# Swapping two steps of a gated-linear-attention chain and the two half banks of PSUM behind them

## Chip, core and metric

The kernel runs on one core of one Trainium2 chip. The metric is the device time of one execution in microseconds; the time before is the median of three executions.

## What is computed

One decoder layer with two branches side by side, on 1024 prompt tokens and 8 x 8 sample tokens: forgetting attention (with a paged cache of 4096 past tokens per sample) and gated linear attention (GLA), merged by gates. The change lies in the GLA branch. Cut to what matters, per head and chunk of 64 tokens:

```python
q_in, k_in = qc * exp(b), kc * exp(-b)                   # b: running sum of log decay
att = where(causal, q_in @ k_in.T, 0)                    # scores
o   = att @ vc + q_in @ S                                # output, S the 128 x 256 state
S   = exp(b_last) * S + (kc * exp(b_last - b)).T @ vc    # state
y   = rmsnorm(o) * silu(gg)                              # norm over 256, gate
```

## The kernel before, in words

Each engine runs its own list of instructions in order; engines meet at semaphores. `schedule()` writes one list of steps for all engines, and each engine runs its handler for every step that concerns it (`run`). The list mixes three streams: the parts of the weight projections (`z`, 6 matmuls each: a quarter of a 128-row weight tile by one of three token chunks of 384, 384 and 320 columns), the decode attention (`kt` transposes a pair of K pages on VectorE, `sc` 64 small score matmuls, `pt` two transposes on TensorE with a copy on ScalarE, `pv` 64 small matmuls, `new`, `soft`, `exp`, `od` the softmax and output of one sample), and the GLA chain. In `gla_steps()` the chain of a head is a list `slow`, and `mix` puts the same number of projection steps (`quick`) behind each of its members, as far as they divide evenly. Some of these have no TensorE part (`evac`, `ev_y`, `ev_z`: sigmoid work on ScalarE and VectorE), so a slot can hold nothing for TensorE.

The chain of head i, block t (128 tokens, two chunks), is

- `att`: TensorE writes the scores (L2028) into bank 7, columns 0 to 127. VectorE masks them in two operations, a minimum (L1826, reads the bank, signals `att_min`) and a maximum (L1828, signals `att_set`).
- `u`: TensorE writes the two state updates (L2035) into columns 0 to 255 of banks 2 and 7. It waits for `att_min` of this block, for `gated` of the block before and for the old state. VectorE folds them into the state (L1843, two operations).
- `o`: TensorE writes the output (L2042, L2045) into bank 7, columns 256 to 511. ScalarE squares and sums it (L1644) and makes the factor of the norm (L1646, L1648).
- `on`: VectorE scales the output into `o_n` (L1849, signals `on_set`).
- `og`: TensorE turns `o_n` (two transposes, L2053) into bank 2, columns 256 to 511; VectorE multiplies both halves with the gate (L1863, L1865, signals `gated`).

After eight blocks come the steps of the sample tokens: `satt` (VectorE first copies q into `q_sp`, L1873, four operations; TensorE writes scores, L2060; VectorE masks them and spreads the keys, L1878), `so`, `son`, `sog`. Also on VectorE's list stand the splitting of each weight tile into a high and a low part (L264, behind ScalarE's L259; it is run at part 1 of the first chunk of a tile, so at every step `z` n 0 1) and L1671, the transposition of K pages.

Semaphore names as used below: `on_set`, `gated`, `att_min`, `qd_set` (the copies into `q_sp`). "Head 1 block 6" counts from 0.

## Time and profile before

| | us |
|---|---|
| median of three executions | 1595.02 |
| lowest, highest of the three | 1590.8, 1600.67 |
| the profiled execution | 1588.89 |
| its span in the profile | 1587.2 |
| TensorE busy in it | 1447.4 (91%) |
| VectorE busy | 726.3 (46%) |
| ScalarE busy | 565.3 (36%) |

The span is the time between the first and the last instruction of the profiled execution; its own time is 1.7 us more. The profiled execution is faster than any of the three that the median is taken over. The GLA chains of the four heads run from 553 to 656, 745 to 858, 949 to 1050 and 1139 to 1233 us of the span.

### The profile page before, as it was taken

How to read it: one execution, taken by the hardware profiler on the slowest of the kernel's cores; microseconds unless marked ns; L12 is line 12 of the kernel's file. 1: busy time of each engine (PE TensorE's matmuls, PEld its weight loads, DVE VectorE, ACT ScalarE, POOL GpSimd, SP SyncE). 2: the span in 40 equal slices, each digit the busy share in tenths (PEclk: the TensorE clock that was granted, in tenths of full speed). 3: DMA queues.
4: the chain of work that ended last, by engine and by line, in shares of the span. 5: the costliest groups of instructions: out<-in, count | busy, mean ns of one | idle time of the engine just before them, and what ended most of it. 6: DMA issues, size and time to landing. Idle time of an engine off the chain costs nothing. (4 is left out here: it accounts for less than half of the span.)

```text
span 1587.2 us, 43486 instructions
## 1 busy us (share of the span) xinstructions
PE 1447.4 (91%) x16281; PEld 1226.6 (77%) x16281; DVE 726.3 (46%) x1578; ACT 565.3 (36%) x1311; POOL 528.7 (33%) x953
## 2 busy tenths in 40 slices
PE   5999898989978897999989999889998899999998
PEld 5878777777767876788877888768876798888876
DVE  4344353543636555655546545655554223333221
ACT  6343444444532334323443334423334353111100
POOL 4444434440047135344353534454251122111000
PEclk9989999999989999999999999989999999999999
DMA  5131301222238688899997999879985764321521
GB/s 173 32 85 34 85 24 54 72 58 68 55 114 212 189 233 216 225 238 235 239 248 206 263 244 243 219 217 244 231 198 158 224 249 139 108 101 62 167 92 60
DMA packets 153411, 250.51 MB, mean 158 GB/s; under 512 B 45897, under 2 KB 58826, under 8 KB 152690
## 3 DMA queue, kind: packets, MB, share of 16 engines
q1 hardware_dynamic: 121618, 215.68, 49.8%
q0 software_dynamic: 31584, 32.04, 7.3%
q8 instruction: 131, 2.15, 0.6%
q14 instruction: 78, 0.64, 0.1%
HBM read 217.37 MB, written 30.22 MB: 156 GB/s over the span
## 5 line engine op out<-in xcount | busy, mean ns | idle before, releaser
L289 PE MATMUL psum<-h_hi,w_hi 128*128 128x384 f32 (+1 forms) x1344 | 491.0, 365 | 13.8 <-DVE q_fm L915 3.5
L289 PE MATMUL psum<-h_hi,w_lo 128*128 128x384 f32 (+1 forms) x1344 | 446.9, 332 | 0.0
L289 PE MATMUL psum<-h_lo,w_hi 128*128 128x384 f32 (+1 forms) x1344 | 446.4, 332 | 0.0
L1457 POOL DMA_DIRECT2D sc<-tmp_bias x512 | 278.3, 549 | 256.7 <-PE psum L1943 252.6
L289 PEld LDWEIGHTS psum<-h_hi,w_hi 128*128 128x128 f32 x1344 | 258.3, 192 | 67.1 <-issue 48.0
L289 PEld LDWEIGHTS psum<-h_lo,w_hi 128*128 128x128 f32 x1344 | 259.4, 193 | 2.7 <-issue 0.5
L289 PEld LDWEIGHTS psum<-h_hi,w_lo 128*128 128x128 f32 x1344 | 257.9, 192 | 0.0
L678 POOL DMA_DIRECT2D lfp<-in_cache_logf x256 | 124.1, 485 | 176.1 <-issue 176.1
L1671 DVE STREAM_TRANSPOSE k_page<-k_page 128x1024 f32<-128x1024 f32 x128 | 156.1, 1232 | 28.8 <-DMA k_page<-in_cache_k 27.8
L264 DVE TENSOR_TENSOR w_lo<-w_raw,w_hi 128x1024 fp32r<-128x1024 f32 x63 | 76.8, 1219 | 110.6 <-ACT w_hi L259 110.5
L259 ACT ACTIVATE w_hi<-w_raw 128x1024 fp32r<-128x1024 f32 x63 | 66.1, 1049 | 69.3 <-DMA w_raw<-in_w_tiles 37.9
L1958 PE MATMUL psum<-v_page,p_t 128*32 128x64 f32 x4096 | 75.2, 227 | 9.8 <-issue 9.6
L1958 PEld LDWEIGHTS psum<-v_page,p_t 128*32 128x32 f32 x4096 | 63.9, 114 | 24.3 <-issue 23.9
L1924 PEld LDWEIGHTS psum<-k_page,q_row 128*32 128x32 f32 x4096 | 64.8, 116 | 22.6 <-issue 22.2
L1924 PE MATMUL psum<-k_page,q_row 128*32 128x64 f32 x4096 | 75.5, 229 | 5.5 <-issue 5.4
L2376 PE MATMUL psum<-o_hi,w_hi 128*128 128x384 f32 (+1 forms) x192 | 69.1, 360 | 0.0
L2368 PE MATMUL psum<-fox_o,up_a 128*128 128x384 f32 (+1 forms) x192 | 62.5, 468 | 0.4 <-issue 0.4
L2376 PE MATMUL psum<-o_hi,w_lo 128*128 128x384 f32 (+1 forms) x192 | 62.6, 326 | 0.0
L2376 PE MATMUL psum<-o_lo,w_hi 128*128 128x384 f32 (+1 forms) x192 | 62.6, 326 | 0.0
L813 ACT ACTIVATE prob<-prob,nmin 128x128 f32<-128x128 f32 (+7 forms) x64 | 49.5, 773 | 36.1 <-DVE nmin L955 36.1
L2291 ACT ACTIVATE h_hi<-g_pair 128x384 fp32r<-128x384 f32 (+1 forms) x24 | 12.1, 505 | 133.2 <-DVE g_pair L2325 133.2
L124 ACT ACTIVATE sig<-sig 128x384 f32<-128x384 f32 (+1 forms) x54 | 27.2, 504 | 90.2 <-DVE sig L130 90.2
(259 smaller groups left out, 2142.4 us busy)
## 6 DMA issues: line engine op xcount, KB each, us to landing
k_page<-in_cache_k SPq DMA_DIRECT2D x256, 256.0 KB, 3.8
v_page<-in_cache_v SPq DMA_DIRECT2D x256, 256.0 KB, 4.9
w_raw<-in_w_tiles SPq DMA_DIRECT2D x63, 512.0 KB, 5.6
g_pair<-tmp_gates SPq DMA_DIRECT2D x16, 544.0 KB, 4.6
sc<-tmp_bias POOLq DMA_DIRECT2D x512, 16.0 KB, 4.4
tmp_ogla<-gate POOLq DMA_DIRECT2D x4, 1088.0 KB, 6.8
g_pair<-tmp_ogla SPq DMA_DIRECT2D x8, 544.0 KB, 7.3
x_in<-in_x_prompt SPq DMA_DIRECT2D x8, 512.0 KB, 6.1
```

The costliest lines, as they stand in the source:

```text
L124: inc(act.activation(g, g, ACT.Exp), "g_sig")
L259: act.activation(self.hi[:, k % 2], self.raw[:], ACT.Copy).then_inc(self.hi_set, 1)
L264: dve.tensor_tensor(self.lo[:, k % 2], self.raw[:], self.hi[:, k % 2].bitcast(F32), ALU.subtract).then_inc(self.lo_set, 1)
L289: m = pe.matmul(out, wt[:, s, k, :], h[:, k, t0:t0 + w], start=(k == 0 and a == 0), stop=(k == KT_ - 1 and a == 2))
L678: pool.dma_start(lfp[a % P:a % P + 1, a // P, :], ins["cache_logf"][ds(page, 1)] .rearrange("o p h -> o (p h)")).then_inc(lf_in[a // P], 16)
L813: inc(act.activation(p, p, ACT.Exp, bias=nmin[:, t % 2, hh:hh + 1], scale=-1.0, accum_out=den[:, t % 2, hh:hh + 1]), "exp_set")
L1457: pool.dma_start(dst, src.unsqueeze(0).to_broadcast([TS, 2, 256])).then_inc(sc_in[j % SLOTS], 16)
L1671: inc(dve.transpose(both, both), "kt_set")
L1924: m = MM(bank[4 + e][32 * hp:32 * hp + 32, col:col + HD].rearrange("p (g t) -> p g t", g=2), q_row[:, b, :], k_page[:, slot:slot + 2, 32 * ...
L1958: m = MM(bank[6][32 * hp:32 * hp + 32, e * HD:(e + 1) * HD], p_t[:, g % 2, col:col + 32], v_page[:, g % 2, tb, h * HD:(h + 1) * HD], start ...
L2368: m = pe.matmul(bank[2 + c][:, 0:w], up_a[:, j % 2, k, :], fox_o[:, k, t0:t0 + w], start=(k == 0), stop=(k == NA - 1))
L2376: m = pe.matmul(bank[5 + c][:, 0:w], wt[:, s, k, :], v[:, k, t0:t0 + w], start=(k == 0 and a == 0), stop=(k == NBR - 1 and a == 2))
```

## The change

The order of the steps: the scores of block t+1 (for the last block: of the sample) stand before the turning of block t. The positions in the list stay, so the projection steps between them stay where they are too; `att` and `og` exchange their places. The output `o` goes to bank 2, columns 256 to 511, and the turned output to bank 7, columns 256 to 511. TensorE's waits follow: `att` waits for `gated` of block t-2 in place of the norm; `og` of block t waits in addition for `att_min` of block t+1; `satt` waits for `gated` of block 6, no longer of block 7.

```diff
-        chain = [[((name, i, t), cost) for name, cost in (("att", 0.3), ("u", 0.55), ("o", 1.0), ("on", 0), ("og", 0.25))] for t in range(TT)]
-        sample = [(("satt", i), 0.3), (("so", i), 1.3), (("son", i), 0), (("sog", i), 0.25)]
+        chain = [[(("att", i, 0), 0.3)]] + [[] for t in range(TT)]
+        for t in range(TT):
+            chain[t] += [(("u", i, t), 0.55), (("o", i, t), 1.0), (("on", i, t), 0)]
+            chain[t].append((("att", i, t + 1) if t < TT - 1 else ("satt", i), 0.3))
+            chain[t + 1].append((("og", i, t), 0.25))
+        sample = chain[TT] + [(("so", i), 1.3), (("son", i), 0), (("sog", i), 0.25)]
...
             def ostat(i, t):
                 W(act, "ot_mm", i, t)
-                inc(A(o_n[:], bank[7][:, DV:2 * DV], ACT.Square, accum_out=ost[:, 0:1]), "ss_set")
+                inc(A(o_n[:], bank[2][:, DV:2 * DV], ACT.Square, accum_out=ost[:, 0:1]), "ss_set")
...
             def o_norm(i, t):
-                inc(dve.tensor_scalar(o_n[:], bank[7][:, DV:2 * DV], ost[:, 2:3], None, ALU.mult), "on_set")
+                inc(dve.tensor_scalar(o_n[:], bank[2][:, DV:2 * DV], ost[:, 2:3], None, ALU.mult), "on_set")
...
             def og(i, t):                                   # VectorE
-                    turned = bank[2][:, DV + j * P:DV + (j + 1) * P]
+                    turned = bank[7][:, DV + j * P:DV + (j + 1) * P]
...
             def att_step(i, t):                             # TensorE
-                W(pe, "on_set", i, t)
+                W(pe, "gated", i, max(t - 1, 0))
                 inc(MM(bank[7][:, 0:P], k_in[:, tok], q_in[:, tok], start=True, stop=True), "att_mm")
...
             def o_step(i, t):
-                o = bank[7][:, DV:2 * DV]
+                o = bank[2][:, DV:2 * DV]
...
             def og(i, t):                                   # TensorE
                 W(pe, "on_set", i, t + 1)
+                W(pe, "att_min", i, min(t + 2, GTS))
-                    m = pe.transpose(bank[2][:, DV + j * P:DV + (j + 1) * P], o_n[:, j * P:(j + 1) * P], cc("ident"))
+                    m = pe.transpose(bank[7][:, DV + j * P:DV + (j + 1) * P], o_n[:, j * P:(j + 1) * P], cc("ident"))
...
             def satt(i):
-                W(pe, "gated", i, TT)
+                W(pe, "gated", i, TT - 1)
...
             def so(i):
-                o = bank[7][:, DV:2 * DV]
+                o = bank[2][:, DV:2 * DV]
```

Five stretches of the list, in the order before; the change exchanges the two steps in brackets and leaves all others (`z` n c p: tile n, chunk c, part p).

```
head 0, blocks 3, 4:  o 3; pt; pv; z 0 1; ev_y; on 3; z 0 2; [og 3]; ev_z; kt; z 0 3; [att 4]; kt; z 1 0; u 4
head 0, blocks 6, 7:  z 0 1; kt; o 6; ev_y; z 0 2; on 6; ev_z; kt; [og 6]; z 0 3; sc; [att 7]; z 1 0; evac; u 7
head 1, blocks 6, 7:  o 6; z 2 1; on 6; z 2 2; [og 6]; kt; z 2 3; kt; z 0 0; [att 7]; sc; z 0 1; u 7
head 1, sample:       on 7; z 1 0; od; kt; z 1 1; [og 7]; ev_y; kt; z 1 2; [satt]; ev_z; sc; z 1 3; so
head 3, blocks 2 to 7: on 2; z; ev_y; pv; [og 2]; z; z; kt; [att 3]; u 3; kt; z 0 0; sc; o 3; evac; on 3; z 0 1;
                      [og 3]; ev_y; [att 4]; z 0 2; pt; u 4; pv; o 4; z; on 4; z; [og 4]; pt; [att 5]; evac; u 5;
                      sc; z; o 5; on 5; new; z; [og 5]; ev_z; soft; pv; [att 6]; z; u 6; z; pt; pv; o 6; on 6; z;
                      [og 6]; [att 7]; ev_y; u 7
```

## Rows read from the trace of the kernel before

**Rows 1.** The waits of PE, whole span: us in total, times, longest.

```profile
...
PE psum L2053 <- DVE o_n L1849: 14.7, 14, 3.4
...
PE psum L2035 <- DVE con L1826: 4.9, 6, 2.4
...
PE psum L2060 <- issue: 3.9, 2, 2.1
...
PE psum L2060 <- DVE q_sp L1873: 2.1, 1, 2.1
...
```

**Rows 2.** Busy time, clock and DMA of two stretches (the columns stand in the first line).

```profile
core 0: us, PE busy (x) PEld busy (x) DVE busy (x) ACT busy (x) POOL busy (x), PEclk, DMA share, GB/s
1046.00:1139.00 93.00, 89.43 (x1486) 79.14 (x1485) 51.47 (x102) 29.41 (x71) 40.24 (x74) 0.96 0.93 235
1139.00:1233.00 94.00, 81.06 (x1291) 61.84 (x1288) 47.70 (x124) 36.67 (x107) 24.39 (x45) 0.96 0.73 184
```

**Rows 3.** Timeline, head 3, blocks 3 and 4: start, us, engine, line.

```profile
...
1182.85 0.65 PE L2045 MATMUL psum<-state,q_in 128*64 128x256 f32 x4
...
1184.68 0.48 DVE L1849 TENSOR_SCALAR o_n<-psum,ost 128x256 f32<-128x256 f32 x1 [2.47 <-issue]
...
1185.31 0.41 PE L2053 MATMUL psum<-con,o_n 128*128 128x128 f32 x2 [0.54 <-DVE o_n L1849]
...
1186.90 1.22 DVE L264 TENSOR_TENSOR w_lo<-w_raw,w_hi 128x1024 fp32r<-128x1024 f32 x1 [1.73 <-ACT w_hi L259]
...
1189.25 0.29 DVE L1826 TENSOR_TENSOR con<-psum,con 128x128 f32<-128x128 f32 x1 [0.21 <-DVE sig L130]
...
1189.60 0.70 PE L2035 MATMUL psum<-gv_tok,gk_tok 64*128 64x256 f32 x4 [2.38 <-DVE con L1826]
...
```

**Rows 4.** Timeline, head 0, block 6.

```profile
...
631.76 1.24 DVE L1671 STREAM_TRANSPOSE k_page<-k_page 128x1024 f32<-128x1024 f32 x1
...
633.60 0.48 DVE L1849 TENSOR_SCALAR o_n<-psum,ost 128x256 f32<-128x256 f32 x1 [0.23 <-DVE sig L130]
...
634.23 0.66 PE L2053 MATMUL psum<-con,o_n 128*128 128x128 f32 x2 [3.43 <-DVE o_n L1849]
...
638.01 0.49 PE L2028 MATMUL psum<-q_in,k_in 128*128 128x128 f32 x2
...
```

**Rows 5.** Timeline, head 1, block 7 and the sample's scores.

```profile
...
843.40 0.48 DVE L1849 TENSOR_SCALAR o_n<-psum,ost 128x256 f32<-128x256 f32 x1 [3.20 <-ACT ost L1648]
...
848.65 0.41 DVE L1873 COPY q_sp<-q_in 128x32 f32<-128x32 f32 x4
...
849.16 0.66 PE L2060 MATMUL psum<-q_sp,k_in 128*64 128x128 f32 x2 [2.14 <-DVE q_sp L1873]
...
```

**Rows 6.** Timeline, other waits of PE, and one turning with its gate.

```profile
...
601.61 0.41 PE L2053 MATMUL psum<-con,o_n 128*128 128x128 f32 x2 [1.20 <-DVE o_n L1849]
...
604.29 0.70 PE L2035 MATMUL psum<-gv_tok,gk_tok 64*128 64x256 f32 x4
...
833.10 0.41 PE L2053 MATMUL psum<-con,o_n 128*128 128x128 f32 x2 [1.10 <-DVE o_n L1849]
...
833.81 0.34 DVE L1865 TENSOR_SCALAR gate<-psum,vec 128x128 f32<-128x128 f32 x1
...
835.26 0.38 PE L2028 MATMUL psum<-q_in,k_in 128*128 128x128 f32 x2
...
1039.90 0.50 PE L2060 MATMUL psum<-q_sp,k_in 128*64 128x128 f32 x2 [2.13 <-issue]
...
```

**Rows 7.** Three stretches behind a wait, columns as in rows 2.

```profile
...
634.50:637.00 2.50, 2.50 (x20) 2.06 (x22) 1.22 (x3) 0.15 (x1) 1.33 (x3) 0.50 0.47 157
849.70:853.20 3.50, 3.50 (x72) 3.03 (x71) 2.37 (x8) 0.00 (x0) 0.49 (x1) 0.62 0.85 242
1040.30:1045.20 4.90, 4.90 (x83) 2.78 (x82) 1.82 (x7) 0.00 (x0) 0.14 (x1) 0.50 0.78 206
...
```

**Rows 8.** The waits of DVE from 550 to 1240 us.

```profile
...
DVE k_page L1671 <- DMA k_page<-in_cache_k: 8.2, 9, 2.1
...
```

## Prediction

> **What bounds the kernel now.** I read the page first: TensorE is busy for 1447.4 of 1587.2 us, VectorE for 726.3. What can be gained without taking matmuls away is TensorE's idle time. The waits of TensorE come second [rows 1]: the turning (L2053) waited 14 times for the norm, 14.7 us in all; the state update (L2035) 6 times for the mask's minimum, 4.9 us; the sample's scores (L2060) three times, 3.9 + 2.1 = 6.0 us. One of the 14 norm waits, 2.7 us, is the sample's own (`sog` of head 3), which the change leaves alone. So 12.0 + 4.9 + 6.0 = 22.9 us are within its reach. Third the table by stretch [rows 2]: between two GLA chains (1046 to 1139 us) TensorE is busy for 89.4 of 93.0 us, in the chain of head 3 for 81.1 of 94.0. That chain has the fewest projection parts between its steps.
>
> Then the timeline, to see what each wait is made of. In head 3 block 3 the output ends at 1182.85 + 0.65 = 1183.50 and the turning starts at 1185.31: the norm takes 1.81 us from matmul to matmul, and its wait is short, 0.54 us [rows 3]. The long waits have another cause: VectorE works its list in order, and the norm stands in it behind the splitting of a weight tile (1.22 us, which itself waits for ScalarE) and K transpositions (1.24 us each). In head 0 block 6 they push the norm to 633.60, 3.43 us of waiting for a chain whose bare length is 1.81 us [rows 4]. The sample's scores wait for copies (0.41 us) that stand behind a transposition in the same way: they begin at 848.65, long after the norm at 843.40 [rows 5]. VectorE is half idle on average and late at these places.
>
> A wait also costs afterwards. Behind those of 3.43, 2.14 and 2.13 us the granted clock was 0.50, 0.62 and 0.50 for 2.5, 3.5 and 4.9 us, so at or partly at the 1.2 GHz level [rows 7]. The loss is 2.5 x 0.50 = 1.3, 3.5 x 0.38 = 1.3 and 4.9 x 0.50 = 2.5 us.
>
> **What the change adds and removes.** No instruction is added or removed on any engine, and the bytes are the same. TensorE's and VectorE's lists, and the few issues that POOL makes at `att` and `satt` (state in and out, not waited for in these chains), have two steps exchanged. The scores no longer wait for the norm: they and the slot behind them now cover it. Added are two waits. The turning waits for the minimum of the next block's mask, which on VectorE stands behind the norm; queued behind the turning on TensorE are the next projection part and the state update. The state update waits, as before, for the gate of the block before, but that gate now lies one slot ahead of it, not two.
>
> The prices from rows: a projection part is (835.26 - 833.10 - 0.14)/2, about 1.0 us, where 0.14 is what two transposes take of the array when nothing stops them (estimate from the two-part slot of [rows 6]). The minimum is 0.29 us [rows 3]. From the start of the turning to the end of the gate's second operation 833.81 + 0.34 - 833.10 = 1.05 us pass [rows 6]. So a slot with one projection part just covers the gate, and an empty slot leaves 1.05 - 0.41 = 0.64 us of waiting.
>
> Block by block, by the order in the list (section on the change). *Waits that go whole*: head 1 block 6. The norm ends at 832.95, TensorE came at 833.10 - 1.10 = 832.00 [rows 6]. Now it runs scores and two parts first and comes to the turning after 834.0, when norm and minimum (833.3) are over: -1.1. The same order holds for head 2 blocks 4 and 6 (0.26, 0.87) and head 3 block 0 (0.41): together -2.6.
>
> *Waits that go in part*: head 0 block 3 and head 2 block 3 (1.20, 1.29). In the first the norm ends at 601.61 - 0.15 = 601.46 (0.15 us from the norm's end to the turning, as in [rows 3]). The turning can start at 601.8, but the gate now stands on VectorE behind mask (0.6) and one transposition (1.24), and ends at 601.46 + 0.6 + 1.24 + 0.6 = 603.9. The state update starts there; with the wait it had started at 604.29 [rows 6]. So -0.4 each, -0.8, instead of -2.5.
>
> *Head 0 block 6*: norm until 634.08, then a transposition, then the minimum: 634.08 + 1.24 + 0.3 less the overlap = 635.5. TensorE has scores, one part and 64 score matmuls (1.1) and comes at 633.1, so it waits 2.4 us instead of 3.43. The state update then starts at 636.8 to 637.9 (with and without full clock), against 638.01 + 1.5 = 639.5 [rows 4]: -1.6 to -2.7. A wait of 2.4 us is as long as those that brought the clock down, so part of the slow stretch returns behind the update: I take -1.2.
>
> *Sample's scores*: they move ahead of the last turning, and the copies ahead of one or two transpositions. In head 1 the norm ends at 843.88; before the copies VectorE had two transpositions, the gate (0.6), a sigmoid product (0.5) and its own waits, until 848.65 [rows 5]; now transposition, gate and sigmoid product of the last 2.2 us stand behind them, so they end near 849.06 - 2.2 = 846.9. TensorE, which came at 849.16 - 2.14 = 847.0 behind turning and part, comes 1.3 us earlier, at about 845.7, and waits some 1.3 us instead of 2.14. That is -0.8, and with a wait so much shorter I count the slow stretch of 1.3 us as gone: -2.1. In head 2 the copies can't pass the gate multiplications of the projection (1.1 us) and a decode product; the wait is 2.1 us as before [rows 6], the clock likely falls again, but two transpositions (2.4 us) now overlap with the two parts that follow (2.0 us), of which the slow clock takes a part back: -1.3. In head 0 the same with a wait of 1.8 us: -0.6. Together -4.0.
>
> *What gets worse*: blocks 3 and 4 of head 1 have a transposition between mask and gate: the state update comes 0.25 us later each, +0.5. In head 3, blocks 2 to 7, several slots are empty. Block 2's turning is directly followed by the update: wait 0.64 in place of 0.38 plus the order, +0.2. Block 3 is the critical one: scores at 1185.0, but the minimum behind norm and split (until 1188.12 + 0.2) ends at 1188.6. The turning has nothing ahead of it and waits 3.5 us, where before 0.54 and 2.38 us were waited [rows 3]; the update comes at 1190.2 instead of 1189.60, while the slow stretch that followed may move or stay: 0 with 1.5 us to either side. Blocks 4 and 5 add 0.6 and 0.1 (slots without a part). In blocks 6 and 7 ScalarE's exponentials and VectorE's fixed sum of work before the product of decode set the pace as before, so that +0.9 is taken up there. Head 3: 0, from -2 to +3.
>
> Sum: -2.6 - 0.8 - 1.2 - 4.0 + 0.5 + 0 = -8.1 us of 22.9 within reach.
>
> **Does DMA take it back?** Between the chains the mean DMA share is 0.93 [rows 2], which reads as nearly full; yet VectorE waited only 8.2 us in nine waits for K pages from 550 to 1240 us [rows 8], all hidden from TensorE. Pages are loaded when score matmuls free them, so a faster chain asks for them earlier by at most 1%. I take 0.5 us for it, between 0 (all hidden, as these nine) and 8 (every such wait comes on top).
> The Trainium skill ("Perfetto Trace Analysis", section Identifying the Most-Contended Engine) says that the occupancy of the 16 DMA engines misleads and that bytes per second are to be judged; with its aggregate of about 435 GB/s (section Roofline) the 235 GB/s of this stretch leave much room, and the DMA term would be 0 (an estimate by that page). By the share alone the whole gain would be lost. The short waits for pages stand nearer to the page's reading.
>
> So the profiled execution of 1588.89 us becomes about 1588.9 - 8.1 + 0.5 = 1581 us. It was 6 us faster than the median; on the median's footing the forecast is 1595.0 - 7.6, about 1587 us.
>
> **Rivals.**
> *More goes than I count (nearly the whole 22.9 us).* If VectorE's backlog shrinks as a whole because its waits for the turning vanish, all three waits go, and 5 us of slow clock: -25, 1570 us. For it: the scores wait for nothing now. Against: the norm remains in front of the mask on VectorE, and the turning waits for both.
> *The wait only changes its name.* The turning waits for the minimum where it waited for the norm, the update for the gate where it waited for the minimum; VectorE's list has the same sum. Head 3 is such a case by my own working. If heads 0 and 2 behave like it: 0 to -3, 1593 us. DMA as the bound gives the same time.
> *Slower.* The mechanism: the gate now one slot ahead of the state update. It decides where that slot holds less than 1.05 us for TensorE or where VectorE has a transposition between mask and gate. If it bites in 14 of the 28 inner blocks at 0.64 us, that is +9, and two more falls of the clock at 1.3 to 2.5 us make +13, with nothing saved: 1608 us. Against it: most slots hold a part and a `kt` that VectorE has finished.
>
> **Numbers.** Forecast (gain 3 to 15 us) 0.58; name only 0.20; more 0.12; slower 0.10. A measurement of this kernel can tell about 1%, 16 us. Faster by more than that needs nearly all of "more" and some of the forecast's upper end: 0.14. Slower by more than 1% is a part of the last rival: 0.06. Within 1%: 0.80. The range takes the forecast's bounds (-15 to -3), the name-only case and the median's own scatter (1590.8 to 1600.7), so about 5 us on each side: 1575 to 1599 us.
>
> **What would show it.** TensorE's waits at L2053 for `o_n` fall from 14.7 to under 6 us, but new ones for L1826 appear there (about 2.4 us in head 0 block 6, 3.5 in head 3 block 3). L2035 waits for L1865 in place of L1826, 4 to 7 us. The three waits at L2060 stay near 1.8, 1.4 and 2.1 us, now directly behind the last norm. The stretch of head 3's chain keeps its 94 us within 2. I am wrong if L2053's waits for both causes stay above 12 us, or fall below 4, or if TensorE begins to wait for K pages.

## The result and the profile after

| | before | after |
|---|---|---|
| median of 12 executions each, run in turns | 1596.83 | 1585.95 |
| lowest, highest | 1587.23, 1602.16 | 1578.24, 1606.22 |
| profiled execution, its own time | 1588.89 | 1586.29 |
| its span | 1587.2 | 1584.6 |

The ratio of after to before is 0.9939, 95% interval 0.9911 to 0.9967. It leaves out executions more than 1.5% above the fastest of their kernel (here the one of 1606.22), and it isn't the quotient of the two medians, here or below. The same changed kernel was measured twice more beside the experiments: 0.9971 (0.9938 to 1.0004) and 0.9948 (0.992 to 0.9975). The mean of the three is 0.9953, so 7.5 us of 1596. The forecast was 7.6 us, and 1587 us for the median, which came out at 1585.95. The change makes the kernel about half a per cent faster, less than single executions of one kernel differ.

The lines moved by four (from the turning on by five): scores L2032, update L2039, output L2046, turning L2058, sample's scores L2065, the mask's minimum L1830, norm L1853, gate L1867 and L1869, copies into `q_sp` L1877, the decode's score matmuls L1928 (before L1924) and value matmuls L1962 (L1958). First the page of after, its span and the busy times:

```profile
...
span 1584.6 us, 43485 instructions
...
PE 1441.8 (91%) x16281; PEld 1223.6 (77%) x16281; DVE 725.9 (46%) x1578; ACT 565.8 (36%) x1311; POOL 530.7 (33%) x953
...
```

TensorE is busy for 5.6 us less than before (1441.8 against 1447.4) with the same 16281 matmuls, and 2.6 us of span are gone. This pair alone would say that time at the slower clock went. Two more profiles of each kernel (below) don't bear it out: TensorE is busy for 1447.4, 1443.7 and 1440.4 us in before and for 1441.8, 1446.7 and 1447.6 us in after. Next the waits of TensorE of after, from 550 to 1240 us, where the GLA chains lie: us in total, times, longest. They answer to [rows 1], whose waits all lie in this stretch too.

```profile
...
PE psum L2039 <- issue: 7.1, 9, 2.1
...
PE psum L2065 <- issue: 6.2, 4, 2.2
...
PE psum L2058 <- DVE con L1830: 5.6, 4, 3.4
...
PE psum L2058 <- DVE o_n L1853: 2.7, 1, 2.7
...
```

The turning waits for the norm only once, 2.7 us: that is the sample's own turning in head 3, which the change leaves alone. In place of the other thirteen it waits four times for the minimum, 5.6 us. The update waits 7.1 us. The view calls this "issue"; by the timeline the gate's last operation is what each of these updates follows. The sample's scores wait in all four heads, 6.2 us. Here are the same sums for the three profiles of each kernel that I have by the end (before: the one of the prediction and two more; after: the first and two repeats), with the 0.2 us of "issue" at the turning:

| waits of TensorE, 550 to 1240 us | before | after |
|---|---|---|
| turning, norm or minimum | 14.7, 15.9, 17.2 | 8.5, 10.0, 9.9 |
| update | 4.9, 5.3, 5.3 | 7.1, 7.4, 6.1 |
| sample's scores | 6.0, 6.2, 6.0 | 6.2, 6.2, 6.2 |
| sum | 25.6, 27.4, 28.5 | 21.8, 23.6, 22.2 |
| score and value matmuls of the decode | 10.0, 11.7, 10.2 | 16.5, 11.1, 16.7 |
| all waits of TensorE | 51.6, 56.1, 53.6 | 53.4, 51.0, 58.1 |

At the three places on which the change acts, 27.2 us become 22.6 on average. The decode's own matmuls wait 4.1 us longer, and the sum of all waits is the same, 53.8 and 54.2 us. So by these profiles TensorE doesn't wait less in this stretch; the chain gets through it faster, as the table of the chains shows below.

The place that the forecast held for the worst is head 3 block 3, here in the timeline of after (start, us, engine, line; in brackets how long the engine waited and for what). It answers to [rows 3].

```profile
...
1179.93 0.38 PE L2032 MATMUL psum<-q_in,k_in 128*128 128x128 f32 x2
...
1182.21 1.22 DVE L264 TENSOR_TENSOR w_lo<-w_raw,w_hi 128x1024 fp32r<-128x1024 f32 x1 [1.73 <-ACT w_hi L259]
...
1183.36 0.28 DVE L1830 TENSOR_TENSOR con<-psum,con 128x128 f32<-128x128 f32 x1
...
1183.74 0.41 PE L2058 MATMUL psum<-con,o_n 128*128 128x128 f32 x2 [3.43 <-DVE con L1830]
...
1185.76 0.63 PE L1947 MATMUL psum<-con,sc 128*128 128x128 f32 x2
...
1186.32 1.22 PE L2039 MATMUL psum<-gv_tok,gk_tok 64*128 64x256 f32 x4
...
```

The scores are done at 1180.3, and the turning stands directly behind them. The minimum that it needs (L1830, 1183.36) is queued behind the split of a weight tile (L264), which itself waited 1.73 us for ScalarE; so TensorE stands for 3.43 us. In before this place cost 0.54 us at the turning and 2.38 at the update. The transposes at 1185.76 take 0.63 us and the update 1.22, where an update takes 0.70 at the full clock.

### The profile page after: what moved, and what is told of

It reads as the page before. It is cut to its first block, busy times and chain, and to the rows that moved or that the text cites. A ratio compares the mean times of both kernels' runs of the same rounds, so it can differ in the third digit from the quotient of the medians.

```text
span 1584.6 us, 43485 instructions
## 1 busy us (share of the span) xinstructions
PE 1441.8 (91%) x16281; PEld 1223.6 (77%) x16281; DVE 725.9 (46%) x1578; ACT 565.8 (36%) x1311; POOL 530.7 (33%) x953
## 4 chain that ended last, share of the span: by engine, by line
PE 54%; issue 5%; DMA 4%; DVE 3%; SPq 2%; ACT 2%; POOL 1%; DVEq 0%; ACTq 0%
PE psum L289 25%; PE psum L2381 6%; PE psum L1962 4%; PE psum L2373 4%; PE psum L1928 4%; PE psum L2411 3%; DMA w_raw<-in_w_tiles 3%; PE psum L2039 1%; PE psum L2046 1%; PE psum L2049 1%; PE psum L1947 1%; SPq L1402 1%; DMA k_page<-in_cache_k 1%; PE psum L2009 1%; PE psum L2420 1%
## 5 line engine op out<-in xcount | busy, mean ns | idle before, releaser
L264 DVE TENSOR_TENSOR w_lo<-w_raw,w_hi 128x1024 fp32r<-128x1024 f32 x63 | 76.8, 1219 | 108.3 <-ACT w_hi L259 108.2
L259 ACT ACTIVATE w_hi<-w_raw 128x1024 fp32r<-128x1024 f32 x63 | 66.1, 1049 | 72.9 <-DMA w_raw<-in_w_tiles 50.2
L1962 PE MATMUL psum<-v_page,p_t 128*32 128x64 f32 x4096 | 73.3, 222 | 14.1 <-issue 14.0
L1962 PEld LDWEIGHTS psum<-v_page,p_t 128*32 128x32 f32 x4096 | 61.9, 111 | 29.1 <-issue 28.8
L1928 PEld LDWEIGHTS psum<-k_page,q_row 128*32 128x32 f32 x4096 | 62.4, 112 | 21.7 <-issue 21.5
L1928 PE MATMUL psum<-k_page,q_row 128*32 128x64 f32 x4096 | 73.1, 224 | 5.0 <-issue 4.8
L1510 ACT ACTIVATE p_t<-psum 128x256 f32<-128x256 f32 x64 | 24.2, 378 | 100.7 <-PE psum L1947 100.7
L2296 ACT ACTIVATE h_hi<-g_pair 128x384 fp32r<-128x384 f32 (+1 forms) x24 | 12.1, 506 | 133.2 <-DVE g_pair L2330 133.2
```

What stands on the lines that cost most here:

```text
L259: act.activation(self.hi[:, k % 2], self.raw[:], ACT.Copy).then_inc(self.hi_set, 1)
L264: dve.tensor_tensor(self.lo[:, k % 2], self.raw[:], self.hi[:, k % 2].bitcast(F32), ALU.subtract).then_inc(self.lo_set, 1)
L1928: m = MM(bank[4 + e][32 * hp:32 * hp + 32, col:col + HD].rearrange("p (g t) -> p g t", g=2), q_row[:, b, :], k_page[:, slot:slot + 2, 32 * ...
L1962: m = MM(bank[6][32 * hp:32 * hp + 32, e * HD:(e + 1) * HD], p_t[:, g % 2, col:col + 32], v_page[:, g % 2, tb, h * HD:(h + 1) * HD], start ...
```

## The experiments

### The kernel again

> The changed kernel, unaltered, for its ratio and a second profile. Theory A (the gain is made inside the four GLA chains; what lies between them is the same work and differs by chance): from the first scores of a head to the start of the sample's output the four chains again take about 12 us less than before (97.8, 108.0, 93.2, 86.9 us became 94.4, 103.4, 90.0, 85.4), while the stretches between them scatter by several us. Theory B (the faster chain is paid back between the chains, by pages or instructions that come late): the stretches after heads 1 and 2 again take 4.2 and 2.6 us more than before. Ratio 0.992 to 0.996 either way.

It was 0.9971 (0.9938 to 1.0004), 1594.49 us against 1596.32, and later

> The changed kernel a third time, for a third profile and to narrow its ratio (0.9939 and 0.9971 so far). Theory A: 0.993 to 0.998, the four chains take 373 to 380 us against 385.9 before, the turning's and the update's waits are the same as in its other two profiles within 1 us each, and what differs from profile to profile is time at the lower clock and pauses within the small page matmuls, which the change does not touch. Rival (the scatter of the profiles comes from the chain's own waits): these waits differ by several us between the three.

0.9948 (0.992 to 0.9975), 1589.11 us against 1597.42. Each ratio lies below 1 (the interval of the first repeat just reaches it) and the three intervals overlap; one alone would have given 5 or 10 us. The first repeat missed its expected 0.992 to 0.996, and its chains took 379.0 us, 7 us less than before and not 12. In the second they took 381.2 us, just above the expected 380, and its updates waited 6.1 us against 7.4, a little outside the 1 us allowed.

Every timed execution comes with its mean granted clock, so the time can be split: span times one minus the clock is what the lower clock took (an estimate), the rest is the span at equal clock. In the first repeat both kernels lost 41.5 us to the clock, and at equal clock the means are 1552.5 us before and 1547.7 after. In the second they lost 42.2 and 38.8 us, and the rest is 1554.0 and 1548.9. So about 5 us (95%: give or take 3) are gained whatever the clock does, and between 0 and 3.4 us more are time at the lower clock.

### The norm's wait given back

```diff
 # att_step, TensorE
                 W(pe, "gated", i, max(t - 1, 0))
+                W(pe, "on_set", i, t)
 # satt
                 W(pe, "gated", i, TT - 1)
+                W(pe, "on_set", i, TT)
```

Order and banks are those of after; only the scores wait for the norm again.

> Order and banks as changed, but the scores (and the sample's) wait for the norm of the block before, as they did. Theory A (the gain is that scores and one slot of projection run while the norm is made): the norm waits return, now at the scores (about 12 us in 13 waits), the turning then waits only for the mask's minimum where its slot is empty, and the gate still lies one slot ahead of the update; so nothing is gained and some is lost: ratio 1.000 to 1.008. Theory C (what helps is the order of VectorE's list, with mask and gate exchanged and the copies earlier): ratio stays at 0.994 to 0.997.

Measured: 1.0048 (1.0019 to 1.0076), 1600.91 us. That is slower than before, and by the ratios 12 us slower than the changed kernel timed beside it (0.9971). Its waits of TensorE, 550 to 1240 us:

```profile
...
PE psum L2033 <- DVE o_n L1853: 13.1, 11, 5.5
...
PE psum L2067 <- DVE q_sp L1877: 6.8, 4, 2.3
...
PE psum L2040 <- issue: 5.2, 8, 1.3
...
```

The norm's waits are back, 13.1 us at eleven scores, the longest 5.5. With them the copies for the sample come late, 6.8 us, and the update keeps 5.2 us of the new wait. With the norm's wait at the scores counted in, TensorE waits 31.1 us at the places of the change, more than before (27.2): it pays for both orders at once. The order of VectorE's list is that of after, so that order by itself gives nothing. What the change gives comes from the scores passing the norm: with that taken away nothing is left.

### The banks alone

```diff
 # the kernel before, with the output in bank 2 and the turned output in bank 7
 # att_step, TensorE
-                W(pe, "on_set", i, t)
+                W(pe, "gated", i, t)
```

> The old order, the new banks: output in bank 2, turned output in bank 7. The scores then must wait for the gate of the block before, which reads bank 7, instead of the norm. Theory A: the banks give nothing by themselves, the norm waits stay at 14 to 15 us, and the wait for the gate costs 0.6 us where scores directly follow the turning (head 3 blocks 3 and 6) and little elsewhere: ratio 1.000 to 1.004. Rival (the exchange of banks helps by itself): below 0.997.

Measured: 1.0012 (0.9982 to 1.0043), 1599.07 us. Its waits of TensorE:

```profile
...
PE psum L2053 <- DVE o_n L1849: 15.7, 14, 6.2
...
PE psum L2028 <- DVE gate L1865: 4.2, 3, 3.0
...
PE psum L2035 <- DVE con L1826: 2.7, 5, 0.8
...
```

The norm's waits stay (15.7 us; [rows 1] had 14.7), and three of 4.2 us come in at the scores, which now wait for the gate that reads bank 7 (forecast were two of 0.6 us; the longest took 3.0, in head 3 block 4). The exchange of the half banks makes nothing faster. It is meant to allow the new order; whether the new order would do as well with the old banks was not tried.

### The sample's scores in their old place

```diff
-            chain[t].append((("att", i, t + 1) if t < TT - 1 else ("satt", i), 0.3))
-            chain[t + 1].append((("og", i, t), 0.25))
-        sample = chain[TT] + [(("so", i), 1.3), (("son", i), 0), (("sog", i), 0.25)]
+            if t < TT - 1:
+                chain[t].append((("att", i, t + 1), 0.3))
+                chain[t + 1].append((("og", i, t), 0.25))
+        chain[TT - 1].append((("og", i, TT - 1), 0.25))
+        sample = [(("satt", i), 0.3), (("so", i), 1.3), (("son", i), 0), (("sog", i), 0.25)]
```

The last turning's wait and that of `satt` were set to fit this order.

> As changed, but the sample's scores stand behind the turning of block 7 again, with their old wait for its gate. Theory A by my sum: 4.0 of the 8 us came from the sample, so the ratio is half way, about 0.997, and the wait at the sample's scores is 2 us in three heads as before. Rival: the sample's new order gave nothing (its waits are 1.9, 1.1, 2.2 and 1.0 us after, against 1.8, 2.1, 2.1 and 0 before), then the ratio is that of the changed kernel, 0.994.

Measured: 0.9983 (0.9957 to 1.0009), 1593.34 us. The sample's scores wait 3.9 + 2.2 us, as in [rows 1]. Against the mean of the changed kernel (0.9953) the sample's part would be 4.8 us of the 7.5, against the changed kernel timed beside it (0.9971) 1.9 us, and my forecast gave it 4.0 of 8.1. With intervals of 0.003 to either side neither nothing nor nearly all of the gain is excluded. The expectation of 0.997 is met, but its rival is not out.

### The split of a weight tile later

In head 3 block 3 and head 0 block 6 the split of a weight tile (1.22 us and what ScalarE needs for its part, L259) stands on VectorE ahead of what TensorE waits for. These runs put it one token chunk later, in both orders of the chain, and the load of the next tile with it.

```diff
 # SyncE: the load of a raw tile
-                if c == 1 and part == 1:
+                if c == 2 and part == 0:
 # ScalarE and VectorE: split_hi, split_lo
-                if c == 0 and part == 1:
+                if c == 1 and part == 1:
```

> The changed kernel with the splitting of each weight tile (ScalarE L259, VectorE L264) moved in the GLA stage from part 1 of a tile's first chunk to part 1 of its second, and the load of the next tile from there to part 0 of the third. Theory A (VectorE's list is the limit: norm and mask stand behind the split): the turning's wait for the mask in head 3 block 3 falls from 3.4 us to under 1, the one of head 0 block 6 from 1.3 to about 0, the sample's of head 3 from 2.7 to under 1; with the slow clock behind them 5 to 9 us less than the changed kernel, ratio 0.989 to 0.993. Rival (another step of VectorE's list takes the split's place, or the next tile's projection now waits for its low part): as the changed kernel, 0.995 to 0.997.

> The same move of the splitting in the kernel before, without the change. Theory A: the long norm waits (3.4, 1.2, 1.3, 0.9 and the sample's 2.7 us) and the update's 2.4 us shrink to the bare chain's 0.3 to 0.5, together 8 to 10 us, so ratio 0.992 to 0.995, and what the change adds to it is smaller than without the move (under 5 us), because half of what it hid was the split. Rival (the change hides the bare norm chain, the split matters little): ratio 0.998 to 1.001, and the change on top of it is worth its full 7 us.

Measured: with the change 0.9891 (0.9853 to 0.9929), 1586.18 us; without it 0.9929 (0.9899 to 0.996), 1587.95 us. The waits of TensorE in the first of the two:

```profile
...
PE psum L2039 <- issue: 11.8, 9, 6.3
...
PE psum L2058 <- DVE con L1830: 1.1, 2, 0.7
...
PE psum L2058 <- DVE o_n L1853: 0.5, 1, 0.5
...
```

The waits at the turning are nearly gone: 1.1 us for the minimum (5.6 before the edit), 0.5 for the norm. In the kernel before, the same edit brings the norm wait of head 0 block 6 from 3.43 us to 0.48, so the split was behind that one too. But the update has 11.8 us, one of them 6.3, in head 1 block 6: there VectorE comes to the split while ScalarE still works at the sample's exponentials, and everything behind the split waits with it. So I left the split early for tiles that have such a step in between:

```diff
+        split_at = {}
+        for n in range(len(tiles)):
+            a, b = steps.index(("z", n, 0, 1)), steps.index(("z", n, 1, 1))
+            split_at[n] = (0, 1) if any(st[0] == "exp" for st in steps[a:b]) else (1, 1)
...
-                if c == 1 and part == 1:
+                if (c, part) == split_at[n]:
```

> The changed kernel with the late split, except for the tiles during whose first chunk ScalarE's exponentials of a sample (about 5 us) begin: these keep the old place. Theory A (the new wait of 6.3 us for the gate in head 1 block 6, seen with the late split, is VectorE standing at the split behind those exponentials): that wait falls to 2 us or less, the other waits stay as with the late split, and the stage takes about 4 us less than with it: ratio 0.985 to 0.989. Rival (the gate there waits for ScalarE's sigmoids, which are late in any case): the wait stays above 4 us and the ratio is that of the late split, 0.989 to 0.992.

> The kernel before with the same selected places of the split. Theory A: as the late split in it, 0.991 to 0.994, since its long wait there was less; the change on top is then worth 3 to 7 us. Rival (without the split in front of the norm the swap has nothing left to hide): the same ratio as with the change.

Measured: 0.9967 (0.9945 to 0.9989), 1590.89 us, and without the change 1.0013 (0.9985 to 1.0042), 1596.92 us. Both missed. The waits of TensorE with the change:

```profile
...
PE psum L2043 <- issue: 7.6, 9, 2.1
...
PE psum L1932 <- issue: 7.9, 3, 5.0
...
PE psum L2062 <- DVE con L1834: 3.8, 3, 2.7
...
```

The 6.3 us at the update did fall to 2.1, as expected. But both kernels with selected places show a new pause of TensorE at the decode's scores near 730 us, 5.0 us here and 5.1 without the change. The edit makes it itself: it loads every tile later, and the tiles that keep the early split then come too late. ScalarE waits for the weight tile (`w_raw`) for 5.9 and 6.1 us at that place and for 11.2 and 12.0 near 915 us; how such a wait reaches TensorE is shown under *DMA* below. So the miss says nothing against the split's part in the waits.

The waits at the three places come to 21.1 us with the change and 19.6 without it when the split is late everywhere, and to 19.4 and 20.2 with selected places. So once the split is out of the way the change saves no waiting in the profiles. By the timed pairs it is still worth 0.004 (0.9891 against 0.9929, which their intervals don't separate) and 0.005 (0.9967 against 1.0013, just clear of them). Whether its worth there is under 5 us, as I expected, is not settled, and neither is whether moving the split helps: I don't offer it as a better version.

### The kernel before, looked at twice more

A place by place comparison needs to know how far two profiles of the same kernel differ.

> The kernel before, unaltered, for a second profile. Theory A (the gain is inside the chains): first scores of a head to the sample's output take 384 to 390 us over the four heads, against 373.2, 379.0 and 381.2 in the changed kernel's three profiles, and all the rest of the span scatters around 1205 us as in those (1205.5 to 1212.0). Theory B (the rest is longer with the change, because pages come late): the rest stays near 1201.3 us as in the first profile, below all three of the changed kernel.

> The kernel before, unaltered, for a third profile; as for the second.

1589.58 and 1583.13 us, spans 1587.9 and 1581.5. Neither theory came out as put. The chains took 380.8 and 380.4 us, below the expected 384 to 390; the rest took 1207.1 and 1201.1 us, once above the lowest of the changed kernel (1205.5) and once at the value of the first profile. The waits of TensorE in the second one:

```profile
...
PE psum L2053 <- DVE o_n L1849: 17.2, 15, 5.0
...
PE psum L2035 <- DVE con L1826: 5.3, 6, 2.4
...
PE psum L2060 <- issue: 3.9, 2, 2.1
...
PE psum L2060 <- DVE q_sp L1873: 2.1, 1, 2.1
...
```

The waits are those of [rows 1] within 2.5 us. What differs is the clock behind them. Here are three windows of this kernel, each 3.5 us from the end of a wait (the columns are those of [rows 2]: width and busy time, granted clock, DMA share, GB/s): behind 4.98 us in head 0 block 6, behind 2.14 in head 1 at the sample, behind 2.39 at the update of head 3 block 3.

```profile
...
634.50:638.00 3.50, 3.49 (x47) 3.06 (x51) 1.51 (x3) 0.84 (x2) 1.62 (x3) 0.50 0.94 206
848.50:852.00 3.50, 3.50 (x82) 2.57 (x86) 2.38 (x8) 0.00 (x0) 1.03 (x2) 1.00 1.00 271
1187.20:1190.70 3.50, 3.34 (x76) 2.15 (x77) 1.23 (x3) 0.52 (x3) 2.88 (x6) 1.00 0.38 121
...
```

In the profile that I predicted from, the clock behind the second was 0.62 over its first 3.5 us by [rows 7] (0.54 in the window laid as here), and 0.60 behind the third. Here both are at the full 1.00. The chain of head 3 took 83.8 us in this profile and 83.7 in the other look, against 86.9 in the first.

### Head 3 in the old order

```diff
+        swap = i < GH - 1
...
+            pair = [(("att", i, t + 1) if t < TT - 1 else ("satt", i), 0.3), (("og", i, t), 0.25)]
+            first, second = pair if swap else pair[::-1]
+            chain[t].append(first)
+            chain[t + 1].append(second)
```

Banks and waits of head 3 are the old ones too.

> As changed in heads 0 to 2; head 3 with the old order, banks and waits. Theory A (the swap pays where each slot holds a projection part, and costs where slots are empty, as in head 3: its chain took 86.9, 83.7, 83.8 us before and 85.4, 86.4, 86.4 with the change): head 3 takes 83.5 to 85.5 us at full clock, the other heads stay at 97, 103.6 and 91, and the whole is 1 to 2 us faster than the changed kernel: ratio 0.993 to 0.996. The waits in head 3 are again those of before (turning 0.3 to 1.0 each, update 2.4 in block 4). Rival (head 3 differs only by the clock in those profiles): no gain, ratio 0.995 to 0.998, head 3 at 85 to 87.

Measured: 0.9978 (0.9957 to 0.9999), 1592.43 us against 1594.87, no better than the change in all four heads (0.9953). Theory A missed; the rival's ratio and its 85 us for head 3 were met. The waits of TensorE:

```profile
...
PE psum L2065 <- DVE o_n L1856: 5.5, 6, 2.7
...
PE psum L2065 <- DVE con L1833: 4.8, 2, 4.6
...
PE psum L2045 <- issue: 5.7, 5, 4.2
...
```

Head 3 brings its norm waits back (5.5 us), and its chain takes 85.0 us: between the old order (83.7 to 86.9) and the new (85.4 to 86.4). The two longest waits are not in head 3 but at places that this run leaves as changed: 4.6 us at the turning of head 0 block 6 and 4.2 us at the update of head 1 block 6. Over all profiles with the new order there and the split where it was, these two places range from 1.3 to 4.6 and from 0.95 to 4.2 us. Giving head 3 its old order gains nothing that can be measured.

### The chains of all profiles

From the first scores of a head to the start of its sample's output, from the timelines, in us; "rest" is the span less the four.

| kernel | head 0 | head 1 | head 2 | head 3 | sum | at equal clock | rest | ratio |
|---|---|---|---|---|---|---|---|---|
| before | 97.8 | 108.0 | 93.2 | 86.9 | 385.9 | 373.5 | 1201.3 | 1 |
| before, look 1 | 97.9 | 106.3 | 92.8 | 83.7 | 380.8 | 375.0 | 1207.1 | 1 |
| before, look 2 | 98.6 | 105.3 | 92.8 | 83.8 | 380.4 | 375.1 | 1201.1 | 1 |
| after | 94.4 | 103.4 | 90.0 | 85.4 | 373.2 | 368.1 | 1211.4 | 0.9939 |
| after, again | 98.7 | 103.4 | 90.6 | 86.4 | 379.0 | 368.8 | 1205.5 | 0.9971 |
| after, third | 97.4 | 103.9 | 93.5 | 86.4 | 381.2 | 367.5 | 1212.0 | 0.9948 |
| scores wait for the norm | 99.4 | 105.4 | 95.5 | 87.4 | 387.7 | 377.5 | 1202.8 | 1.0048 |
| banks alone | 98.2 | 106.2 | 94.8 | 89.7 | 388.9 | 377.4 | 1207.2 | 1.0012 |
| sample in its old place | 96.3 | 106.5 | 90.4 | 87.6 | 380.8 | 372.9 | 1218.0 | 0.9983 |
| head 3 in the old order | 97.4 | 107.1 | 91.4 | 85.0 | 380.9 | 369.0 | 1208.9 | 0.9978 |
| before, split late | 92.2 | 113.5 | 90.4 | 88.0 | 384.1 | 373.4 | 1202.2 | 0.9929 |
| after, split late | 90.4 | 114.3 | 97.8 | 86.5 | 389.0 | 377.0 | 1199.9 | 0.9891 |
| before, split selected | 91.8 | 108.3 | 90.6 | 87.4 | 378.1 | 375.7 | 1214.1 | 1.0013 |
| after, split selected | 93.4 | 112.4 | 91.3 | 84.0 | 381.1 | 372.6 | 1205.8 | 0.9967 |

Each row is one execution. "At equal clock" is the sum less what the lower clock took in each chain (its length times one minus its mean granted clock, an estimate from the trace). As they stand the chains shrink by 4.6 us on average (382.4 to 377.8): heads 0 to 2 by 1.3, 2.9 and 1.6, and head 3 grows by 1.3. The lower clock took 12.4, 5.8 and 5.4 us of them in before and 5.1, 10.2 and 13.7 in after. Taken off, what is left repeats within 1.6 us in each kernel and shrinks by 6.4 us, from 374.5 to 368.1: by 3.5 us in head 0, 0.3 in head 1, 2.5 in head 2 and 0.1 in head 3. This is the clearest reading of the change in the profiles. Without the passing of the norm (scores wait, banks alone) it is gone.

The rest of the span scatters by 6 to 7 us within one kernel and is longer in after, 1209.6 against 1203.2 us on average, so that the three profiled executions of after are 1.9 us longer as a whole (spans of 1587.4 against 1585.5). The timed executions say the opposite, and the profiles of before are the odd ones: at equal clock their spans are 1542 to 1547 us, where 96 timed executions of that kernel lie at 1545 and above, most near 1553. Why they are so fast isn't known. So what the change does outside the chains can't be read from these profiles. In the four kernels with a moved split neither the raw chains nor those at equal clock follow the ratios.

## Why the prediction was right

The time: 7.6 us forecast, 7.5 measured. The mechanism, scores that pass the norm, holds, and the waits went and came where the forecast had them. Some terms were mis-sized, to both sides. Most stretches of the chain repeat within 0.1 us from profile to profile, so the forecast can be set against them place by place: from the end of a block's output to the next update (for the sample: to its output), the means of three profiles of each kernel.

| places | forecast | measured |
|---|---|---|
| waits that go whole (four) | -2.6 | -3.5 |
| waits that go in part (two) | -0.8 | -1.1 |
| head 0 block 6 | -1.2 | -3.0 |
| the sample's scores (four heads) | -4.0 | -1.6 |
| head 1 blocks 3 and 4 | +0.5 | +0.5 |
| head 3 blocks 2 to 6 (forecast: 2 to 7) | 0 | +2.1 |
| head 1 block 5, head 2 block 5 | none | -0.6, -1.1 |

The stretches between update and output, which I took as unchanged, grow by 2.7 us in sum on average: the lower clock takes 3.4 us of them in after and 0.4 in before. Point by point:

*Waits that go whole.* Shown. In head 1 block 6 the turning came without waiting, as in the other three places of that group. But just ahead of it the update of the same block, which had waited 0.22 us (0.53 and 0.55 in the other two profiles), now waits for the gate of block 5. Here are the steps that make it late, in the timeline of after:

```profile
...
816.96 0.49 ACT L113 ACTIVATE sig<-psum 128x384 f32<-128x384 f32 x1
...
818.60 0.56 DVE L130 SCALAR_TENSOR_TENSOR sig<-psum,sig 128x384 f32<-128x384 f32 x1 [0.98 <-ACT sig L117]
...
819.68 0.34 DVE L1869 TENSOR_SCALAR gate<-psum,vec 128x128 f32<-128x128 f32 x1
...
820.12 0.70 PE L2039 MATMUL psum<-gv_tok,gk_tok 64*128 64x256 f32 x4 [2.06 <-issue]
...
```

The gate (L1869) stands on VectorE behind a sigmoid product (L130), which waits 0.98 us for ScalarE, whose list has the sample's exponentials and copies ahead of that sigmoid. The gate ends at 820.02 and the update starts at 820.12, after 2.06 us (2.33 and 0.95 in the other two profiles). My step "a slot with one projection part just covers the gate" looked at the array's side and at transpositions on VectorE, not at a third engine behind VectorE. This step of the working was wrong: TensorE waits 1.8 us there on average where it had waited 0.4. It cost no time in these profiles, for from the output of block 5 to this update it is 12.1, 10.6 and 10.7 us in before and 10.4, 10.4 and 10.9 in after. In before a pause of 2.2 to 2.8 us in the decode's matmuls ahead of it was followed by the lower clock, in after one of 1.7 to 2.0 us by the full clock in two of three. By the same profile a slot without a part costs 0.75 us, where I had 0.64.

*Head 0 block 6.* Forecast 2.4 us of waiting instead of 3.43. Measured 1.31, 2.80 and 2.75 (before 3.43, 3.69, 4.98). Right in kind; the gain at this place was more than twice the 1.2 us that I took, in part because the one profile that I predicted from has the shortest wait of the three. Likewise head 2 block 5 had a norm wait of 0.94 us in both looks and none in that first profile, so the forecast doesn't have it.

*The sample's scores.* Forecast waits of 1.8, 1.3 and 2.1 us in heads 0 to 2; measured 1.86, 1.14 and 2.19 in the first profile, and 0.97 in head 3, which the forecast didn't have. Their sum hardly changes (6.0 to 6.2), as forecast. What I had too large is what lies behind them: from the end of the last output to the sample's output the four heads take 34.6, 33.4 and 31.5 us in before and 30.5, 32.2 and 32.1 in after, so 1.6 us less and not 4.0. In head 1 it is 1.65 us less, in head 2, where I had 1.3 us for transpositions that overlap, 0.3 us more. The timed run with the sample in its old place gives 2 or 5 us for the same term, with an interval that holds both. The place in head 1, to set beside [rows 5], in the timeline of after:

```profile
...
828.03 0.38 PE L2032 MATMUL psum<-q_in,k_in 128*128 128x128 f32 x2
...
830.20 0.38 PE L2058 MATMUL psum<-con,o_n 128*128 128x128 f32 x2
...
841.81 0.40 PE L2065 MATMUL psum<-q_sp,k_in 128*64 128x128 f32 x2 [1.14 <-issue]
...
```

The first two rows are the scores of block 7 and, behind them, the turning of block 6: no wait, where [rows 6] had 1.10 us. The third is the sample's scores, 1.14 us instead of 2.14.

*Head 3.* Forecast 0 for its blocks 2 to 7, from -2 to +3, with a wait of 3.5 us at block 3. The wait is 3.43 us in all three profiles of after. The chain grows by 1.3 us on average, which is as much as the lower clock takes more of it: in the two looks at before, where the clock stayed at 1.00 throughout, it took 83.7 and 83.8 us, in the three of after 85.4 to 86.4 with a mean clock of 0.98, 0.98 and 0.96, and at equal clock the means are 83.9 and 83.8. Two waits of 0.54 and 2.38 us, the second of which is followed by the full clock in two of three profiles, are gathered into one of 3.43, which was followed by the lower clock every time. That one stands ahead of the update, so a projection part and the update itself run slowly on the chain's way. From the end of the output to the next update it is 7.50 us in after (1178.82 to 1186.32; 6.77 and 7.85 in the other two), 6.10 in before (1183.50 to 1189.60, and the same in the looks). My step had 6.7 and left the clock to "may move or stay": that is the other 0.7 us on average.

*The clock.* Mis-sized. I counted the slow stretch behind head 1's wait as 1.3 us that go for certain. In before the same 2.14 us were followed by a clock of 0.54, 0.67 and 1.00, so it was at stake in two of three executions. Behind the 1.14 us of after it was 1.00 in all three. That stretch did go, but it is no net gain of the change: others came back elsewhere, and over the four chains the lower clock took 7.9 us in before and 9.7 in after on average. The windows of 3.5 us from the end of a wait, of after: head 0 block 6 (waited 1.31), head 1 sample (1.14), head 2 sample (2.2), head 3 block 3 (3.43).

```profile
core 0: us, PE busy (x) PEld busy (x) DVE busy (x) ACT busy (x) POOL busy (x), PEclk, DMA share, GB/s
645.10:648.60 3.50, 3.49 (x72) 3.15 (x76) 3.01 (x8) 1.54 (x3) 0.00 (x0) 1.00 1.03 200
841.80:845.30 3.50, 3.49 (x78) 3.04 (x79) 3.02 (x9) 0.52 (x1) 3.43 (x7) 1.00 1.10 194
1030.80:1034.30 3.50, 3.50 (x13) 3.17 (x14) 2.77 (x8) 0.56 (x2) 2.79 (x6) 0.55 1.10 211
1183.70:1187.20 3.50, 3.46 (x14) 2.70 (x14) 1.28 (x4) 0.85 (x2) 1.64 (x4) 0.56 0.13 47
...
```

The first two are at the 2.4 GHz level, the last two partly or mainly at 1.2 GHz. Head 0 block 6 had 0.50 to 0.56 in all three profiles of before. In after it had 1.00 only in this first profile, behind 1.31 us; in the two repeats, behind 2.80 and 2.75 us, it was 0.50 and 0.55. That part of the slow stretch would return behind a wait of 2.4 us was in the forecast.

*DMA.* I took +0.5 with bounds 0 and 8. Its size stays open. VectorE's waits for K pages, 550 to 1240 us, were 8.2, 13.5 and 10.2 us in before, 15.4, 9.9 and 24.1 in after. The longest wait of TensorE in the third profile of after, 5.25 us at 738 us, comes from DMA too, but not from a K page, as I had on my list: it comes from a weight tile, by way of two engines.

```profile
...
728.05 1.06 ACT L259 ACTIVATE w_hi<-w_raw 128x1024 fp32r<-128x1024 f32 x1 [7.38 <-DMA w_raw<-in_w_tiles]
729.14 1.23 DVE L264 TENSOR_TENSOR w_lo<-w_raw,w_hi 128x1024 fp32r<-128x1024 f32 x1 [4.35 <-ACT w_hi L259]
...
731.76 0.51 ACT L1542 ACTIVATE sc<-sc,smst 128x256 f32<-128x256 f32 x1 [2.65 <-DVE smst L1704]
...
736.90 1.09 ACT L1510 ACTIVATE q_row<-psum 32x128 f32<-32x128 f32 x4
...
738.09 1.94 PE L1928 MATMUL psum<-k_page,q_row 128*32 128x64 f32 x64 [5.25 <-issue]
...
```

The tile came 13.4 us after its issue (4.2 to 7.6 us for the same tile in the other five profiles), while the DMA engines moved 239 GB/s, the rate of the stretch in [rows 2] where the forecast saw room. ScalarE waited for it, VectorE's split for ScalarE, the sample's exponentials (L1542) for VectorE, and TensorE's scores for the copy of q (L1510) behind them, which ended at 737.99. The K pages were turned at 736.70. It happened in one of three executions of after, the slowest of its profiles. I can't say whether the change brings it. The mean stretch between the chains of heads 1 and 2 is 100.0 us in after and 97.5 in before, which fits a little of the gain being paid back, and is no proof.

*The sum.* As they stand the chains gave 4.6 us instead of 8.1. At equal clock they gave 6.4, where the forecast without its 1.3 us of clock is 6.8. By head the forecast had -2.2, -2.7, -2.8 and -0.4; measured at equal clock are -3.5, -0.3, -2.5 and -0.1. Head 1 is the one that is far off, as half of its forecast was the clock and of the other 1.4 us only 0.3 came. The timed executions give 7.5 us by the ratios, of which some 5 at equal clock. So the mechanism and the order of size are right, while too small terms (head 0 block 6, two places not forecast) made up for too large ones (the sample, head 3). That the forecast met the time within 0.1 us is luck, as single ratios of this kernel range from 5 to 10 us.

*The rivals.* "Nearly the whole" is out: 22.6 us of the waits are left, where it wanted almost none, and the time is far from the 1570 us it gave. "The wait only changes its name" holds for head 3, and at equal clock for head 1. "Slower" had its mechanism right, as the updates wait 6.9 us for the gate where they had waited 5.2 for the minimum, and its count wrong: 9 places and not 14, most of them short. Of the signs that I set, the turning's waits lie where they should (8.3 to 9.8 us, between 4 and 12; the norm's part 2.7, under 6), the update's at the upper end (6.1 to 7.4, forecast 4 to 7).

## What to carry to other kernels

When a producer's result waits in another engine's in-order list, moving an independent matmul group ahead of its consumer covers the latency only as long as the next consumer down the chain still has a slot of its own; follow the chain one engine further than the wait that is removed. One long wait can cost more than two short ones: in head 3, 0.54 and 2.38 us became 3.43, the clock fell behind it each time, and from one output to the next it went from 9.3 to 9.9 us to 11.0 to 12.2. A new wait need not cost time (the 1.4 us more at head 1 block 6 didn't); look how long the stretch around it takes. And a change of half a per cent is settled by timed pairs. Profiles explain it better when the time at the lower clock is taken off first.

## What the runs showed of the hardware that was not expected

The granted clock behind a wait is not a function of the wait. The same 2.14 to 2.16 us before the sample's scores of head 1 were followed by 0.54, 0.67 and 1.00; waits of 2.38 to 2.39 us in head 3 by 0.60, 1.00 and 1.00; those of 1.8 to 1.9 us in head 0 by 1.00, 0.69 and 1.00 before and 1.00, 0.71 and 0.53 after. Over all fourteen profiles, 550 to 1240 us, the clock of the next 3.5 us was 1.00 behind 40 of 46 waits of 1.2 to 1.5 us, behind 11 of 41 of 2.0 to 2.3 us, and behind none of the 22 of 3.43 us and more (0.50 to 0.69). With the sample's last steps included the four chains lost some 15, 13 and 7 us so in before and 5, 11 and 14 in after: a scatter as large as the effect of the change. The Trainium skill ("TensorE: Matmul & The Clock Gate", What's actually happening) ties the clock to how busy TensorE has been recently and says that the moment of a change varies from run to run with where a free-running watch happens to stand. The traces fit it: the same gap of 2.14 us sometimes cost a slow stretch and sometimes nothing.

TensorE also pauses within groups of 64 small decode matmuls for up to 3.6 us with no releaser in the profile ("issue"). The pause comes at the same matmul of the group each time, its length does not repeat: ahead of the 23rd near 624 us it took 1.5 to 3.2 us in the six profiles of the two kernels, ahead of the 40th near 815 us 1.7 to 2.8. Two others come and go: ahead of the 37th near 915 us it took 3.6 and 3.4 us in two profiles of after, 0.9 in two of before, and was missing in the third of each; ahead of the 49th near 1110 us it took 3.3, 2.8 and 1.5 us in after and 2.2 in one profile of before. What they are was not tried.
